# Low parts of the weights moved from VectorE to GpSimd, and a causal mask added in PSUM by VectorE

## What is computed

```python
x = x + 0.5 * swiglu(rms_norm(x, ffn1_norm), ffn1_w_gate, ffn1_w_up, ffn1_w_down)
x = x + hybrid_mixer(rms_norm(x, mix_norm), positions, ...)
x = x + 0.5 * swiglu(rms_norm(x, ffn2_norm), ffn2_w_gate, ffn2_w_up, ffn2_w_down)
y = rms_norm(x, norm_final)

# in the mixer: latent attention, 8 heads, causal, in blocks of 128 queries
logits = einsum("bqhd,bkhd->bhqk", qb, k) * scale
logits = where(k_pos[None, :] <= q_pos[:, None], logits, -1e30)
p = softmax(logits);  out = einsum("bhqk,bkhd->bqhd", p, v)
# and dilated attention, 3 groups of 8 heads with a bias table; both branches are
# gated with sigmoids, added, and multiplied by w_out
```

## Time and profile before

| | |
|---|---|
| time, median of 3 runs | 1284.85 us (1284.72 to 1285.17) |
| the profiled execution: its own time | 1285.54 us |
| the profiled execution: span of the core | 1283.7 us |
| granted TensorE clock, mean | 0.999 of full speed |
| PE busy | 1270.7 us (99%) |
| DVE busy | 669.6 us (52%) |
| ACT busy | 442.9 us (35%) |
| POOL busy | 18.8 us (1%) |

### The profile page before, as it was taken

The page is one execution under the profiler, slowest core; times in us unless marked ns, Lnnn a source line. Parts: engine busy times, 40 slices in busy tenths (PEclk is TensorE's granted clock), DMA queues, the critical chain, the costliest instruction groups (busy, mean ns, idle before and its releaser), DMA issues.

```text
span 1283.7 us, 16607 instructions
## 1 busy us (share of the span) xinstructions
PE 1270.7 (99%) x5998; PEld 1031.0 (80%) x5998; DVE 669.6 (52%) x984; ACT 442.9 (35%) x763; POOL 18.8 (1%) x36
## 2 busy tenths in 40 slices
PE   9999999999999999999999999999999999999997
PEld 6788888888888777787878878788888888888886
DVE  5744444433336777575655747676644444443323
ACT  5333322322233445343343424423433322332221
POOL 0000000000000000300000000000000000000000
PEclk9999999999999999999999999999999999999999
DMA  6342223333322221522222121223222223233321
GB/s 213 99 112 98 98 98 98 90 91 94 102 92 71 64 69 66 131 67 82 81 73 93 65 92 56 83 97 99 99 98 98 98 98 98 95 86 96 93 89 65
DMA packets 36003, 118.38 MB, mean 92 GB/s; under 512 B 4680, under 2 KB 4680, under 8 KB 35968
## 3 DMA queue, kind: packets, MB, share of 16 engines
q1 hardware_dynamic: 34416, 114.83, 27.6%
q0 software_dynamic: 1264, 3.06, 1.4%
q10 hardware_dynamic: 288, 0.03, 0.0%
HBM read 115.36 MB, written 2.55 MB: 92 GB/s over the span
## 4 chain that ended last, share of the span: by engine, by line
PE 94%; DVE 2%; DMA 1%; issue 1%; ACT 1%; SPq 0%; DVEq 0%; ACTq 0%
PE bank L540 36%; PE bank L374 17%; PE bank L376 17%; PE bank L375 17%; PE bank L723 1%; PE bank L746 1%; PE bank L643 1%; PE bank L670 1%; DMA x<-in_x_t 1%; DVE mla_stats L1445 1%; PE bank L763 1%; PE bank L659 1%; PE bank L759 1%; ACT w_hi L356 0%; PE bank L732 0%
## 5 line engine op out<-in xcount | busy, mean ns | idle before, releaser
L361 DVE TENSOR_TENSOR w_lo<-raw,w_hi 128x1024 fp32r<-128x1024 f32 (+2 forms) x221 | 258.8, 1171 | 228.8 <-ACT w_hi L356 226.7
L356 ACT ACTIVATE w_hi<-raw 128x1024 fp32r<-128x1024 f32 (+2 forms) x221 | 224.3, 1015 | 429.7 <-PE bank L540 228.3
L540 PE MATMUL bank<-act_hi,w_hi 128*128 128x512 f32 x704 | 217.8, 391 | 1.6 <-DVE act_lo L1170 0.8
L540 PE MATMUL bank<-act_hi,w_lo 128*128 128x512 f32 x704 | 216.9, 389 | 0.0
L540 PE MATMUL bank<-act_lo,w_hi 128*128 128x512 f32 x704 | 216.8, 389 | 0.0
L374 PE MATMUL bank<-act_hi,w_hi 128*128 128x512 f32 x528 | 212.0, 401 | 2.0 <-DVE w_lo L361 1.2
L376 PE MATMUL bank<-act_hi,w_lo 128*128 128x512 f32 x528 | 206.2, 391 | 0.0
L375 PE MATMUL bank<-act_lo,w_hi 128*128 128x512 f32 x528 | 205.8, 390 | 0.0
L540 PEld LDWEIGHTS bank<-act_hi,w_hi 128*128 128x128 f32 x704 | 131.6, 188 | 31.7 <-DVE w_lo L361 2.6
L540 PEld LDWEIGHTS bank<-act_hi,w_lo 128*128 128x128 f32 x704 | 132.1, 188 | 27.7
L540 PEld LDWEIGHTS bank<-act_lo,w_hi 128*128 128x128 f32 x704 | 132.1, 188 | 27.4
(11 more groups left out here) (177 smaller groups left out, 1052.5 us busy)
## 6 DMA issues: line engine op xcount, KB each, us to landing
raw<-in_ffn_up SPq DMA_DIRECT2D x87, 512.0 KB, 3.3
raw<-in_w_dil SPq DMA_DIRECT2D x40, 512.0 KB, 3.3
raw<-in_ffn_down SPq DMA_DIRECT2D x32, 448.0 KB, 3.3
raw<-in_ffn_down SPq DMA_DIRECT2D x16, 512.0 KB, 3.5
raw<-in_w_mla_gates SPq DMA_DIRECT2D x8, 512.0 KB, 3.3
raw<-in_w_branches SPq DMA_DIRECT2D x8, 512.0 KB, 3.2
raw<-in_w_out SPq DMA_DIRECT2D x8, 512.0 KB, 3.3
raw<-in_w_latent SPq DMA_DIRECT2D x6, 512.0 KB, 3.2
```

Source lines behind the costliest of these rows:

```text
L356: nc.scalar.activation(w_hi[:, s % SPLIT, 0:tiles * P], raw[:, s % RAW, 0:tiles * P], ACT.Copy).then_inc(hi_ready, 1)
L361: nc.vector.tensor_tensor(w_lo[:, s % SPLIT, 0:tiles * P], raw[:, s % RAW, 0:tiles * P], w_hi[:, s % SPLIT, 0:tiles * P].bitcast(F32), ALU ...
L540: last = nc.tensor.matmul(out, w[:, s % SPLIT, tile * P:(tile + 1) * P], moving[:, row, :], start=row == 0 and w is w_hi and moving is act_hi,
```

## The change

1. `split_lo` goes from DVE to GpSimd for every piece but the first three. GpSimd's program becomes a list of 219 subtractions in the order of the pieces.
2. The skewed bias table was stored and read back by DMAs on GpSimd's queue. Both now stand on SP's queue: the store after the loads of the first three up turns, the 24 reads after the load of dilated piece 2.
3. The mask matmuls (L645), four a head, go. DVE adds the mask to the four diagonal blocks in PSUM before the maxima, and waits for these adds (its own semaphore) before it reduces. The two rounded copies of identity and mask, and PE's wait for them, go.
4. In the first turn the load of piece 2 is issued before that of x's last chunk, and ACT's `split_hi` of piece 4 comes ahead of its Silu. In the last head `split_hi` of dilated piece 1 comes ahead of the exponentials.

```diff
-        def split_lo(dve, s, d, tiles):
-            dve.wait_ge(hi_ready, s + d + 1)
-            nc.vector.tensor_tensor(w_lo[:, s % SPLIT, 0:tiles * P], raw[:, s % RAW, 0:tiles * P],
+        def split_lo(engine, operations, s, d, tiles):
+            engine.wait_ge(hi_ready, s + d + 1)
+            operations.tensor_tensor(w_lo[:, s % SPLIT, 0:tiles * P], raw[:, s % RAW, 0:tiles * P],
                                     w_hi[:, s % SPLIT, 0:tiles * P].bitcast(F32),
                                     ALU.subtract).then_inc(lo_ready, 1)
...
+            def store_skew():
+                sp.wait_ge(rows_ready, 1)
...
+            def load_biases():
+                sp.wait_ge(skew_stored, 16)
+                sp.wait_ge(piece_done, PIECES["mla"] + 2 * MLA_HEADS - 1)
...
             for k in range(HALF, KM):
                 sp.wait_ge(x_loaded[k - HALF + 1], 16)
+                if k == KM - 1:
+                    load(sp, 2, 0, ffn[0][0][2], TILES)
                 load_x(k)
...
+            pool.wait_ge(lo_ready, 3)
+            split_up(0, 3)
+            split_down(0)
...
+            for phase in ("merge", "out"):
+                with pool.Fori(0, KM // 4) as i:
+                    for q in range(4):
+                        split(PIECES[phase] + q, 4 * i, TILES)
+            split_up(1, 0)
+            split_down(1)
...
-                    nc.tensor.matmul(out, mla_q[0:QK_DIM, h % 2, b * P:(b + 1) * P],
-                                     mla_k[0:QK_DIM, h % 2, 0:(b + 1) * P], start=True, stop=False, skip_group_check=True)
-                    last = nc.tensor.matmul(diagonal, mask_ident[:, :], mask_causal[:, :], start=False, stop=True,
-                                            skip_group_check=True)
+                for b, out in enumerate((bank[2][:, 0:P], bank[3][:, 0:2 * P], bank[2][:, P:SEQ], bank[4][:, :])):
+                    last = nc.tensor.matmul(out, mla_q[0:QK_DIM, h % 2, b * P:(b + 1) * P],
+                                            mla_k[0:QK_DIM, h % 2, 0:(b + 1) * P], start=True, stop=True, skip_group_check=True)
...
-                    else:
+                    elif not (first and f == 0):
                         split_hi(act, s + 2, 4 * i, TILES)
                     split_hi(act, s + 3, 4 * i, DOWN_PARTS[1][1] - DOWN_PARTS[1][0] if last and j else TILES)
+                    if first and f == 0 and j == 0:
+                        split_hi(act, s + 4, 0, TILES)
...
                 dve.wait_ge(mla_scores, h + 2 * i + 1)
+                dve.wait_ge(const_loaded, 16)
+                for diagonal in (bank[2][:, 0:P], bank[3][:, P:2 * P], bank[2][:, 3 * P:SEQ], bank[4][:, 3 * P:SEQ]):
+                    last = nc.vector.tensor_tensor(diagonal, diagonal, causal, ALU.add)
+                last.then_inc(own, one())
+                dve.wait_ge(own, so_far())
```

More of the change, by code:

```diff
@@ L437, in _, with load_dilated @@
             load(sp, s + 2 * MLA_HEADS - 1, 0, w_mla_gates[MLA_HEADS - 1], TILES)
-            with sp.Fori(0, PAIRS) as i:
+            def load_dilated(i, first=False):
                 for q in range(10):
                     load(sp, PIECES["dil"] + q, 12 * i, w_dil[bass.ds(i, 1), q].rearrange("a p n -> p (a n)"), TILES)
+                    if first and q == 2:
+                        load_biases()
                 last_gate = w_dil[bass.ds(i, 1), 10].rearrange("a p n -> p (a n)")
@@ L443, in _ @@
                     load(sp, PIECES["dil"] + 10 + part, 12 * i, last_gate[:, part * HALF * P:(part + 1) * HALF * P], HALF)
+            load_dilated(0, first=True)
+            with sp.Fori(1, PAIRS) as i:
+                load_dilated(i)
             for phase, source in (("merge", w_branches), ("out", w_out)):
@@ L465, in _, with split @@
             pool.dma_start(t5_rel[:, :], rel_bias).then_inc(table_loaded, 16)
[L467 to L480, removed]
+            def split(s, d, tiles):
+                split_lo(pool, nc.gpsimd, s, d, tiles)
@@ new lines, in split_up, with split_down @@
+            def split_up(f, first):
+                for q in range(first, 4):
+                    split(PIECES[f"up{f + 1}"] + q, 0, TILES)
+                with pool.Fori(0, KF // 2 - 1) as i:
+                    for q in range(4):
+                        split(PIECES[f"up{f + 1}"] + 4 + q, 4 * i, TILES)
+            def split_down(f):
+                with pool.Fori(0, 2) as i:
+                    for q in range(12):
+                        a, b = DOWN_PARTS[q % 3]
+                        split(PIECES[f"down{f + 1}"] + q, 12 * i, b - a)
@@ new lines, in _ @@
+            pool.wait_ge(lo_ready, 3)
+            split_up(0, 3)
+            split_down(0)
+            for q in range(6):
+                split(PIECES["latent"] + q, 0, TILES)
+            with pool.Fori(0, PAIRS) as i:
+                for h in range(2):
+                    split(PIECES["mla"] + 2 * h, 4 * i, LORA_TILES)
+                    split(PIECES["mla"] + 2 * h + 1, 4 * i, TILES)
+            with pool.Fori(0, PAIRS) as i:
+                for q in range(12):
+                    split(PIECES["dil"] + q, 12 * i, TILES if q < 10 else HALF)
@@ L1255, in up_turn @@
                     nc.vector.tensor_tensor(work[:, 0, :], bank[c % UP_BANKS][:, :], rstd[:, :], ALU.mult).then_inc(chunk_taken, 1)
-                    if not (first and f == 0 and j == 0):
-                        split_lo(dve, s + 3, 4 * i, DOWN_PARTS[1][1] - DOWN_PARTS[1][0] if last and j else TILES)
                     dve.wait_ge(silu_ready, hidden + 2 * i + 1)
@@ L1274, in down_turn @@
                 for m in range(4):
-                    for part in range(3):
-                        s = PIECES[f"down{f + 1}"] + 12 * turn + 3 * m + part
-                        if not (final and m == 3 and part == 2) and not (turn == m == part == 0):
-                            following = DOWN_PARTS[(part + 1) % 3]
-                            split_lo(dve, s + 1, 12 * i, following[1] - following[0])
+                    s = PIECES[f"down{f + 1}"] + 12 * turn + 3 * m + 2
                     c = CHUNKS[f"down{f + 1}"] + 4 * turn + m
@@ L1632, in dilated_pair @@
                 for q in range(12):
-                    tiles = HALF if q in (9, 10) else TILES
                     if q == 8:
                         expand_stats(i)
-                    if q > 1 or not first:
-                        split_lo(dve, s + q + 1, d, tiles)
                     if q in (3, 5, 7):
```

76 lines of the change are left out of this document (33 added, 43 removed).

## The result

The changed kernel takes **1298.2 us** (median, 1296.1 to 1298.98), the kernel before 1284.8 us beside it on the same chip (1284.4 to 1285.2). The ratio is **1.0101, 95% interval 1.0089 to 1.0113**: 1% slower, and 6 us above the upper end of the range that was forecast. The profiled execution has a span of 1297.3 us, 13.6 more than before (1283.7), at a mean granted clock of 0.997 (before: 0.999). The four executions of the changed kernel lie 3 us apart, so a single difference of medians against it is good to about 1.5 us; the traces are compared piece by piece for that reason.

A forecast was written before the change was run, and what follows sets the result against it. PE, busy 1270.7 of 1283.7 us, was taken as the bound. Terms -2.7 - 1.2 + 1.9 + 2.1 + 1.4 + 0.6 = +2.1 us on 1285.54 gave 1287.6, set to 1287.0 for the runs' median; 8-in-10 range 1282.5 to 1292.0.

The forecast's parts named there:

- Queues: DMAs moved to SP's queue: the store ahead of piece 12's load, and the bias reads, were to cost 0.
- Rival 2: DVE and GpSimd hold each other up at two-input SBUF work: +1 to +4 us, 1288 to 1291; chance 0.15.
- The start: +0.6: First pieces: 1.2 us wait for piece 3's split, less 0.3 for piece 2's earlier load and 0.3 at piece 4.
- Masks: -2.7: Latent heads: dropping four mask matmuls saves PE 0.34 us a head, eight heads, -2.7 us (-1.8 to -3.5).
- adds in PSUM: +1.9: Latent heads: DVE's mask adds delay the reductions; PE waits 3.3 us at seven gates against 1.4 before, +1.9 us.
- Merge +2.1, out +1.4: In merge and out GpSimd's splits come 0.53 and 0.35 us too late for PE, four times each: +2.1 and +1.4 us.
- the rule of every second piece: In merge and out only every second piece was to pay the late split, the next one's being ready in time.
- Down 0, with 0.14 to spare: Down stages: tightest pieces have 2.43 us for a split needing 2.29, so cost 0 with 0.14 us to spare.
- Last head -1.2: Last latent head: dilated piece 1's rounding ahead of the exponentials removes PE's 1.18 us wait, -1.2 us.
- Dilated 0: Dilated attention: time to hide the splits about as long as in the up stages, so cost 0.
- Rival 1: The hop to GpSimd is longer than priced: merge, out, down and start pay more, 1295 us; chance 0.2.
- Rival 3: Splits need 2.0 us or less, so merge and out cost nothing: 1282.9, or 1281.2 with cheap adds; chance 0.15.

The follow-up runs named there:

- experiment 1: Changed kernel with the skew store on SyncE one turn of loads later, so the loads of pieces 12 to 15 stand ahead of it: 1294.8 us.
- experiment 4: Changed kernel with the first up stage's product of Silu and scale (L1297) reading the scale from PSUM, so one SBUF input instead of two: 1293.3 us.
- experiment 2: Changed kernel with the load of piece 2 behind x's last chunk again, as before the change: 1294.8 us.
- experiment 8: Kernel before, with the last latent head's new order and the 14 splits of latent pieces 2 to 15 on GpSimd, masks on TensorE: 1282.2 us.
- experiment 9: Kernel of experiment 8 with the masks added by VectorE in PSUM instead of on TensorE: 1283.6 us.
- experiment 5: Changed kernel with the four mask matmuls a head back on TensorE: 1295.5 us.
- experiment 3: Changed kernel with the 16 splits from `merge` piece 1 to `up2` piece 0 back on VectorE: 1292.6 us.
- experiment 10: Changed kernel with the alterations of experiments 1 to 4, piece 3's split on VectorE and the masks back on TensorE: 1283.4 us.

## Why the prediction was wrong

- **"Queues: the store on SP stands some 4 us in front of piece 12, which is loaded 8 us before its use: 0" failed, and it is the largest miss, 4.8 us.** It took the time of `t_row` from the trace of before (63.1) and a free queue, and it read the lead of the load wrongly. In the trace of before that load went out at 52.93, 24 us ahead of its first matmul at 77.27. The measured store waited 17.7 us for a `t_row` that came at 68.97, and the load behind it went out 16.8 us later than before and took 10.6 us to land, not 4. Removing either link removes the loss or nearly all of it (experiments 1 and 4). The prediction also had no term for the clock, which makes 1.7 of the 4.8.
- **Rival 2 (VectorE and GpSimd hold each other up) was right in kind and wrong in place.** It said "in the up stages the DVE chain has room for two such waits". That holds for all turns but one: the product takes 2.3 us on average and costs nothing. It fails in the one turn in which VectorE also works out the rotation angles: there the product (L1297), one of the two operations of L1258 and one of the four of L1241 are held up one behind the other, which makes +1.1 us at piece 10 and the late store. The Trainium skill, SBUF — State Buffer, section on who interferes with whom, states that a VectorE instruction with two SBUF inputs contends with a GpSimd instruction that reads SBUF; that one in a two-port mode, which tensor_scalar can enter, and GpSimd block each other for a whole instruction; and that one with at most one SBUF input, outside these modes, does not contend. The trace agrees on all three: 0.69 us becomes 2.4 with two inputs in SBUF; the normalisation's product of 384 columns by a scalar (L1492) takes 1.43 us on average in place of 0.42; and the adds of a mask from SBUF to PSUM take 292 ns, beside a split or not.
- **"The start: +0.6" measured +2.6.** The earlier load of piece 2 was given -0.3 as a gain; it delays x's last chunk by 2.7 us and is a loss of 2.3 (experiment 2). The term of 1.2 us for piece 3's split on GpSimd measured 1.0.
- **"Masks: -2.7" measured -2.8 (3.0 between experiments 8 and 9), "adds in PSUM: +1.9" measured +2.1 over seven heads, and there the sum stopped too early.** The adds themselves were sized right: 0.89 us (0.92 predicted), reductions 1.03 us behind the scores (1.08). The wait at the gates was right too (3.0 against 3.3, of which the move of the splits gives back 1.6 by experiment 8; predicted 1.4). What failed is that the sum ended at the start of the gates. The longer first matmuls (0.8) and the next query (0.3) were left out (experiment 9). So were the transposes behind the last head and those at dilated piece 2, +1.3 and +0.6 us, where PE waits for VectorE's normalisation (0.6 and 0.4 us) and once for the query (0.2). With the masks on TensorE (experiment 5) the first is +0.8 and the second is gone.
- **"Merge +2.1, out +1.4" measured +2.6 and +1.8 (experiment 3).** Mechanism and price are right: 2.60 us from `w_hi` to PE, 2.57 predicted; GpSimd's 1024 columns at 2.40, 2.37 predicted. In `merge` every second piece pays, as forecast, about 0.5 us, and those between 0.17; in `out` each pays 0.23, so there the wait is spread and the rule of every second piece didn't hold. The excess is the longer first matmul after a wait, some 0.1 us in each piece.
- **"Down 0, with 0.14 to spare" held** (+0.2 over down and the projections). **"Last head -1.2"** measured -1.4. **"Dilated 0"** measured +1.2; 0.6 of it is the step at piece 2 named above, the rest is mostly in steps of 0.1 to 0.2 at the tenth piece of each pair. These steps are in experiment 10 and not in experiment 8, so they come with the splits; which operation carries them there was not isolated.
- Rival 1 (a longer hop) is refuted: 0.08 us to GpSimd and 0.05 to 0.13 back. Rival 3 fell with the price of 2.40.

The terms as measured: -2.8 (masks) + 2.1 (adds, seven heads) - 1.4 (last head) + 2.6 + 1.8 (`merge`, `out`) + 2.6 (start) + 1.1 (piece 10) + 4.8 (store, with the clock) + 1.2 (dilated) + 1.3 (transposes behind the last head) + 0.1 = +13.4, against 13.6 in the two spans.

## What to carry to other kernels

When elementwise work moves from VectorE to GpSimd, price first what VectorE is doing meanwhile: every operation of VectorE's with two SBUF inputs, or a scalar product in place, can be held until GpSimd's ends, and shows it as its own duration. Look for the one stretch in which VectorE's queue is full, not at the average piece, and move only the splits whose cover and neighbours allow it. A DMA that waits for a computed result, put ahead of loads in the queue that feeds the bottleneck, makes its wait theirs; put behind enough loads it cost 0.1 us here (experiment 1). A wait of the bottleneck can cost more than its length: look at the granted clock behind it. A chain that is lengthened must be followed to its last reader, beyond the first wait that it causes.

## What the runs showed that was not expected

- A held-up VectorE instruction shows no idle time for it in the profile: L1297 is listed at 2311 ns on average over 44 instructions. In experiment 4 the idle time before one is about 1 us both where it is held (16.1 us for 16) and where it isn't (16.3 for 18). A comparison of mean durations finds it; with one operand in PSUM it was 687 ns beside the same splits.
- A 512 KB load issued just behind the 446.5 KB store landed after 10.6 us with the store on the same queue and after 10.8 with the store on GpSimd's (kernel before), the median load after 3.2.
- A wait of PE of 2.80 us was followed by 3.4 us at a granted clock of 1.2 GHz instead of 2.4, which cost 1.7 us more.
- One load queued 0.36 us ahead of a chunk of x put that chunk back by 2.7 us.
